# A fourth weight slot, a first stage over two token tiles, and later bf16 stores in a fused decoder layer

## The reference

```python
p = x @ w_in      # columns: [B_a | C_a | v_a | val_b | gate_b | g_a | g_b], 1024 each
y_a = (B_a * conv3_causal(C_a * v_a)) @ w_out_a
u   = conv31_causal(val_b * sigmoid(gate_b)) + conv_b_bias
y_b = silu(LN(u)) @ w_out_b
mix = (sigmoid(g_a) * y_a + sigmoid(g_b) * y_b) @ w_o
x1  = LN(alpha * x + mix)
x2  = LN(alpha * x1 + relu(x1 @ w_up)**2 @ w_down)      # output, float32
```

## Time and profile before

| | us |
|---|---|
| median of the runs shown (2359.38, 2360.63, 2711.35) | 2360.63 |
| the profiled execution's own time | 2351.3 |
| its span on the slowest core, number 6 | 2349.8 |
| spans of the 8 cores | 2327.6 to 2349.8 |
| PE busy | 2189.2 (93%) |
| DVE, ACT, POOL busy | 825.3, 901.7, 561.7 |

### The profile page before, as it was taken

The page is one execution under the profiler, slowest core; times in us unless marked ns, Lnnn a source line. Parts: engine busy times, 40 slices in busy tenths (PEclk is TensorE's granted clock), DMA queues, the critical chain, the costliest instruction groups (busy, mean ns, idle before and its releaser), DMA issues.

```text
span 2349.8 us, 33231 instructions; the slowest of 8 cores (2327.6 to 2349.8 us)
## 1 busy us (share of the span) xinstructions
PE 2189.2 (93%) x11616; PEld 968.0 (41%) x11616; DVE 825.3 (35%) x1200; ACT 901.7 (38%) x1424; POOL 561.7 (24%) x501
## 2 busy tenths in 40 slices
PE   5787899989999999999999999999999999999796
PEld 2333344333444434434444444444444444444342
DVE  2342360313703246122542237132461336322403
ACT  1132155222563225522354324723255324642552
POOL 0022041421405303132313214033031323040221
PEclk9899999999999999999999999999999999999898
DMA  9978879798677976657644665447644475444352
GB/s 169 220 207 174 206 164 172 175 243 215 154 198 182 260 216 177 187 175 237 202 151 147 203 199 190 145 157 218 211 155 144 151 225 191 157 152 171 119 187 90
DMA packets 109108, 428.42 MB, mean 182 GB/s; under 512 B 12944, under 2 KB 54160, under 8 KB 66448
## 3 DMA queue, kind: packets, MB, share of 16 engines
q1 hardware_dynamic: 84240, 318.21, 41.6%
q0 software_dynamic: 15488, 91.30, 21.4%
q10 hardware_dynamic: 9216, 16.78, 1.9%
HBM read 437.31 MB, written 63.44 MB: 213 GB/s over the span
## 4 chain that ended last, share of the span: by engine, by line
PE 76%; DMA 17%; DVE 2%; issue 2%; ACT 1%; POOL 1%; SPq 0%; POOLq 0%; DVEq 0%; ACTq 0%
PE ps L260 72%; DMA wsl<-wblk 8%; DMA wbf<-wsl 5%; PE ps L378 4%; DMA rep<-u0d 2%; DMA xft<-xblk 1%; POOL tt L270 1%; DVE res L283 1%; DMA wsl<-wbf 1%; DVE sbf L270 0%; ACT rstd L266 0%; SPq L108 0%; DVE sgt L283 0%; DVE tt L270 0%; DVE rstd L283 0%
## 5 line engine op out<-in xcount | busy, mean ns | idle before, releaser
L260 PE MATMUL ps<-xbf,wsl 128*128 128x512 bf16 x3648 | 844.8, 387 | 71.0 <-DMA wsl<-wblk 58.8
L260 PE MATMUL ps<-bx,wsl 128*128 128x512 bf16 x2560 | 572.5, 381 | 3.0 <-DMA wsl<-wblk 2.8
L260 PEld LDWEIGHTS ps<-xbf,wsl 128*128 128x128 bf16 x3648 | 356.0, 99 | 524.3 <-issue 127.6
L260 PE MATMUL ps<-h,wsl 128*128 128x512 bf16 x2496 | 549.6, 381 | 17.5 <-DMA wsl<-wblk 17.5
L266 ACT ACTIVATE tA<-ps 128x512 f32<-128x512 f32 x448 | 266.3, 595 | 511.2 <-PE ps L260 470.6
L260 PEld LDWEIGHTS ps<-bx,wsl 128*128 128x128 bf16 x2560 | 249.6, 98 | 312.7 <-issue 19.1
L260 PEld LDWEIGHTS ps<-h,wsl 128*128 128x128 bf16 x2496 | 244.5, 98 | 317.6 <-issue 28.3
L270 POOL TENSOR_TENSOR tt<-tt,rstd 128x512 f32<-128x512 f32 x180 | 246.5, 1370 | 97.9 <-ACT rstd L266 75.3
L270 POOL TENSOR_TENSOR tt<-res,mu 128x512 f32<-128x512 f32 x112 | 152.6, 1363 | 462.3 <-DMA yblk<-tt 219.9
L266 ACT ACTIVATE sq<-res 128x512 f32<-128x512 f32 x112 | 69.9, 630 | 412.5 <-DVE res L283 412.5
L270 POOL TENSOR_TENSOR tt<-u,mu 128x512 f32<-128x512 f32 x68 | 92.0, 1354 | 507.6 <-ACT mu L266 452.3
(11 more groups left out here) (54 smaller groups left out, 1010.5 us busy)
## 6 DMA issues: line engine op xcount, KB each, us to landing
wsl<-wbf SPq DMA_DIRECT2D x225, 1024.0 KB, 5.2
wsl<-wblk POOLq DMA_DIRECT2D x63, 1024.0 KB, 11.8
wbf<-wsl SPq DMA_DIRECT2D x36, 1024.0 KB, 12.3
rep<-u0d SPq DMA_DIRECT2D x256, 135.0 KB, 4.1
xft<-xblk POOLq DMA_DIRECT2D x64, 256.0 KB, 7.6
yblk<-tt ACTq DMA_DIRECT2D x64, 256.0 KB, 6.9
u0d<-u SPq DMA_DIRECT2D x64, 136.0 KB, 3.9
xbf<-xblk POOLq DMA_DIRECT2D x8, 1024.0 KB, 12.9
```

Of the source, the lines that this page charges most:

```text
L260: last = e.matmul(bank_ap, lhsT=l, rhs=r, start=(start and idx == 0), stop=(stop and idx == n - 1))
```

## The change

- **Slots.** `NS` is 4: loads are issued up to n+3. The space comes from `u0`, whose 8 tiles with halo give way to 3 tiles in rotation (`NU`) and 2 small halo tiles, and from `sbf`, 4 tiles to 2. `u0d` holds all tokens of a channel in one row, so that the halo of pass i+1 is what pass i wrote; the DVE copy of the halo goes.
- **First stage.** `stage_F_start` runs the F work of passes 0 and 1 on one loading of the B0 blocks, with conv(0, 0 to 5) in between. The first x tile and the first block are loaded in halves, and 16 matmuls on the first halves come first. conv(0, 6), conv(0, 7) and the layer norm of pass 0 go into `stage_S1A(0)`. Pass 0 has no F stage and no B0 loads.
- **Stores.** The 26 other blocks are stored at passes 1 to 3, by a table: 8, 12 and 6. Float32 reads in passes 0 to 3: 26, 26, 18, 6, that is 76 instead of 53.
- **Mix sums.** `stage_mix` uses `Stats`: 14 additions on DVE instead of 8, 2 matmuls instead of 8. The 2 are issued after S1A's first tile (in the last pass, after the first late DN block).
- **Last pass.** `LATE` is 3. `ln1_apply` there writes the residual on DVE. The statistics of pass 6 are issued behind f = 1 of `stage_up`.
- **End.** `ln2_last` works in place instead of through `tt`, subtracts for 5 tiles before it needs 1/sigma, and issues the outputs on SP's queue.

```diff
-NS = 3
+NS = 4
+NU = 3
...
-        LATE = 2
+        LATE = 3
         seq = [B0 + k for k in range(4)] + [A0 + k for k in range(6)]
         for i in range(NPASS):
-            if i < NPASS - 1:
+            if 0 < i < NPASS - 1:
                 seq += [B0 + k for k in range(4)]
...
+        STORE_PASS = (2, 1, 2, 3, 2, 1, 2, 3, 1, 2, 3, 1, 2)
...
-            return blk % 3
+            k = blk - S30 if blk < A0 else blk - UP0 + 10
+            return STORE_PASS[k % 13]
...
+        def F_gate(i, j, bv, bgk):
+            r = rt("sgt", 2)
+            act(sgt[r][:], ps[bgk][:, :], AF.Tanh, reads=[("ps", bgk)], writes=[("sgt", r)], scale=0.5)
+            ru = rt("u0", NU)
+            stt(u0[ru][:], sgt[r][:], 1.0, ps[bv][:, :], ALU.add, ALU.mult,
+                reads=[("ps", bv), ("sgt", r)], writes=[("u0", ru)])
+            rel(bv, bgk)
+            S.dma("sp", udsem[i % 2][j], u0d[j, :, HL + i * T:HL + (i + 1) * T], u0[ru][:],
+                  reads=[("u0", ru)], writes=[("u0d", i % 2, j)])
...
+        def stage_F_start():
+            for m in range(4):
+                s = w_next(B0 + m)
+                js = (2 * m, 2 * m + 1)
+                if m == 0:
+                    bks = [(nb(), nb()) for _ in js]
+                    for j, pair in zip(js, bks):
+                        for which, b in enumerate(pair):
+                            mm(ps[b][:, :], [(wk(s, kc, 2 * j + which), xbf[0][:, kc, :]) for kc in range(4)],
+                               reads=["w0a", "x0a"], writes=[("ps", b)], start=True, stop=False)
+                    for j, pair in zip(js, bks):
+                        for which, b in enumerate(pair):
+                            mm(ps[b][:, :], [(wk(s, kc, 2 * j + which), xbf[0][:, kc, :]) for kc in range(4, 8)],
+                               reads=[("wsl", s), ("xbf", 0)], writes=[("ps", b)], start=False, stop=True)
+                        F_gate(0, j, *pair)
+                        F_halo(j, s)
+                    for j in js:
+                        bv, bgk = nb(), nb()
+                        F_mm(1, j, s, bv, bgk)
+                        F_gate(1, j, bv, bgk)
+                        if j == 1:
+                            spread(0, 0)
+                else:
+                    for j in js:
+                        for i in range(2):
+                            bv, bgk = nb(), nb()
+                            F_mm(i, j, s, bv, bgk)
+                            F_gate(i, j, bv, bgk)
+                            if i == 0:
+                                F_halo(j, s)
+                        if j == 2:
+                            spread(0, 1)
+                        conv(0, j - 2, stC)
...
             if j + NREP < 8:
                 spread(i, j + NREP)
+            elif i == 0:
+                spread(1, j + NREP - 8)
...
+                if late:
+                    tsc("dve", buf[:, e_, :], tt[r][:], pv[:, 3, e_:e_ + 1], pv[:, 4, e_:e_ + 1],
+                        ALU.mult, ALU.add, reads=[("tt", r), "cst"], writes=[(bid, e_)])
...
+        def ln2_last(i, R):
+            buf, bid = R
+            eng = ["pool" if e_ % 3 == 2 else "dve" for e_ in range(7)] + ["pool"]
+
+            def sub(e_):
+                tten(eng[e_], buf[:, e_, :], buf[:, e_, :], mu[1][:], ALU.subtract,
+                     reads=[(bid, e_), ("mu", 1)], writes=[(bid, e_)])
+
+            order = [0, 2, 1, 5, 3, 7, 4, 6]
+            for e_ in (0, 2, 1, 5, 3):
+                sub(e_)
+            for n, e_ in enumerate(order):
+                if e_ in (7, 4, 6):
+                    sub(e_)
+                tten(eng[e_], buf[:, e_, :], buf[:, e_, :], rstd[1][:], ALU.mult,
+                     reads=[(bid, e_), ("rstd", 1)], writes=[(bid, e_)])
+                act(buf[:, e_, :], buf[:, e_, :], AF.Identity, reads=[(bid, e_), "cst"],
+                    writes=[(bid, e_)], bias=pv[:, 6, e_:e_ + 1], scale=pv[:, 5, e_:e_ + 1])
+                S.dma("sp", osem[n % NTT], yblk[i, :, e_, :], buf[:, e_, :],
+                      reads=[(bid, e_)], writes=[("y", i, e_)])
...
-                if e_ % 2 == 0:
-                    prev = (e_, q)
-                else:
-                    p, pq = prev
-                    rs = bf16_sum((rbuf[:, p, :], rbuf[:, e_, :]), [(rid, p), (rid, e_)])
-                    rq = bf16_sum((sq[pq][:], sq[q][:]), [("sq", pq), ("sq", q)])
-                    pend.append((e_ // 2, rs, rq))
...
+                if prev is not None:
+                    st_.take(*prev)
+                prev = (e_, rbuf[:, e_, :], (rid, e_), sq[q][:], ("sq", q))
+            st_.take(*prev)
...
+        stage_F_start()
+        lnc_tasks = [(lambda j=j: lnc_apply(j)) for j in range(8)]
         for j in range(8):
             stage_S1A(0, True, j)
-            conv(0, j, stC)
+            if j < 2:
+                conv(0, 6 + j, stC)
+            elif j == 2:
+                stC.finish(0)
+            else:
+                take(lnc_tasks, 2 if j < 6 else 1)
+        ln_flush()
...
+                if last and f == 1:
+                    stD.finish(1)
```

More of the change, by code:

```diff
@@ L152, in build_nc @@
         apre = sb("apre", [128, 8, T], BF16)
-        u0 = sb("u0", [128, 8, HL + T], BF16)
+        u0 = [sb(f"u0_{i}", [128, T], BF16) for i in range(NU)]
+        u0h = [sb(f"u0h{i}", [128, HL], BF16) for i in range(2)]
         u = sb("u", [128, 8, T], F32)
@@ L157, in build_nc @@
         sumQ = [sb(f"sumQ{i}", [128, T], F32) for i in range(2)]
-        sbf = [sb(f"sbf{i}", [128, T], BF16) for i in range(4)]
+        sbf = [sb(f"sbf{i}", [128, T], BF16) for i in range(2)]
         mu = [sb(f"mu{i}", [128, T], F32) for i in range(2)]
@@ L227, in w_next @@
                 S.dma("sp", castsem[expect], wbf[expect], wsl[n % NS][:],
-                      reads=[("wsl", n % NS)], writes=[("wbf", expect)])
+                      reads=[("wsl", n % NS)] + (["w0a"] if n == 0 else []),
+                      writes=[("wbf", expect)])
             return n % NS
@@ L291, in wk, with F_mm, F_halo, stage_F @@
             return wsl[s][:, kc * 512 + q * 128: kc * 512 + (q + 1) * 128]
-        def stage_F(i, first, each=None):
-            xb = xbf[i % 2]
+        def F_gate(i, j, bv, bgk):
[7 more added lines that the diff above has]
+                  reads=[("u0", ru)], writes=[("u0d", i % 2, j)])
+        def F_mm(i, j, s, bv, bgk):
+            q0 = (j % 2) * 2
+            for which, b in ((0, bv), (1, bgk)):
+                mm(ps[b][:, :], [(wk(s, kc, q0 + which), xbf[i % 2][:, kc, :]) for kc in range(8)],
+                   reads=[("wsl", s), ("xbf", i % 2)], writes=[("ps", b)])
+        def F_halo(j, s):
+            q0 = (j % 2) * 2
+            hv, hg = nb(), nb()
+            for which, b in ((0, hv), (1, hg)):
+                mm(ps[b][:, 0:HL], [(wk(s, kc, q0 + which), xhbf[:, kc, :]) for kc in range(8)],
+                   reads=[("wsl", s), "xhbf"], writes=[("ps", b)])
+            rh = rt("hsm", 4)
+            act(hsm[rh][:], ps[hg][:, 0:HL], AF.Tanh, reads=[("ps", hg)], writes=[("hsm", rh)], scale=0.5)
+            ru = rt("u0h", 2)
+            stt(u0h[ru][:], hsm[rh][:], 1.0, ps[hv][:, 0:HL], ALU.add, ALU.mult,
+                reads=[("ps", hv), ("hsm", rh)], writes=[("u0h", ru)])
+            rel(hv, hg)
+            S.dma("sp", uhsem[j], u0d[j, :, 0:HL], u0h[ru][:], reads=[("u0h", ru)],
+                  writes=[("u0dh", j)])
+        def stage_F(i, each):
             s = None
@@ L298, in stage_F @@
                     s = w_next(B0 + j // 2)
-                q0 = (j % 2) * 2
                 bv, bgk = nb(), nb()
[L301 to L318, removed]
@@ L531, in stage_mix @@
                    start=True, stop=False)
[L533 to L537, removed]
             prev = None
@@ L650, in build_nc, with f_each @@
         MER = (h, "h")
[L652 to L653 removed]
+        stage_F_start()
+        lnc_tasks = [(lambda j=j: lnc_apply(j)) for j in range(8)]
         for j in range(8):
             stage_S1A(0, True, j)
[L656 removed]
+            if j < 2:
+                conv(0, 6 + j, stC)
+            elif j == 2:
+                stC.finish(0)
+            else:
+                take(lnc_tasks, 2 if j < 6 else 1)
+        ln_flush()
         ln2_tasks = []
[L659 removed]
         for i in range(NPASS):
             last = i == NPASS - 1
[L662 to L675 removed]
+            if 0 < i < NPASS - 1:
+                def f_each(j):
+                    take(ln2_tasks, 1 if j % 2 else 0)
+                stage_F(i + 1, f_each)
             for e_ in range(4):
@@ L726, in build_nc @@
                 stD.finish(1)
-                for e_ in range(8):
-                    ln_flush(1)
-                    ln_fin.append(ln2_apply(i, R, e_, "pool" if e_ % 3 == 2 else "dve"))
-                ln_flush()
+                ln2_last(i, R)
             else:
```

83 lines of the change are left out of this document (32 added, 51 removed).

## The result

Four runs of the changed kernel took 2326.8 to 2336.1 us, median 2332.1, against 2350.4 to 2360.6 us for the kernel before. The ratio is 0.9894, with a 95% interval of 0.9853 to 0.9935: 1.1% faster, 25 us, where 88 were forecast and the range ended at 2325. (Executions far above the others of their kernel, as the 2711.35 us of the kernel before, are left out of all ratios: where their clocks are on record, one die or both ran at a lower one.) The profiled executions differ by less, since that of before was within 1 us of its fastest and that of after was its slowest: their spans are 2349.8 and 2334.6 us.

The account below looks back on a forecast made before the run. The start was taken as bound by transfers, the middle by PE, passes 0 to 2 by something between. Gains of 33 + 36 + 0 + 13 + 6 = 88 us gave 2263 from the profiled 2351.3 (2273 from the median); range 2240 to 2325.

Parts of the forecast that it names:

- Prices of transfers: All-engine time per transfer: 6.45 us a casting load, 3.2 a bf16 block or store; said to hold within 4%.
- slower rival: Casting loads cost some 9 us each in the busy passes; kernel at 2371 us, chance 0.05.
- From need to loss: Passes 0 to 3: transfer need against PE time turned into losses totalling 32 us; 36 us gained.
- the line with three slots: Passes 0 to 3: losses read from the old kernel's transfer shares; new shares would lose 96 us together.
- rate, not slots: Rival for passes 0 to 3: the line of losses holds, passes lose 96 us; kernel at 2337 us, chance 0.13.
- Start: Stretch before S3 of pass 0: S3 begins at 153 instead of 186.5 us; 33 us gained, bounds 22 and 43.
- Mix sums: Mix stage: six matmuls less and six DVE additions more net minus 1 to plus 3 us a pass; taken as 0.
- Late blocks and end: Last pass: a third late DN block and shared work gain 13 us; its end, with fewer waits, gains 6.

Follow-up runs that it names:

- e4: The changed kernel with three weight slots and eight u0 tiles in rotation; 1.0039 of the kernel before.
- e3: The changed kernel with the 26 blocks stored at passes 0 to 2 as before; 0.9785 of the kernel before.
- e13: The changed kernel with the ten B0 and A0 blocks stored at their second use instead of their first; 0.9982 of the kernel before.
- e14: The changed kernel with the edits of e3, e5, e6, e7 and e13 and the mix sums as before the change; 0.9827 of the kernel before.
- e5: The changed kernel with the halo of pass 0 written in one transfer with its u0 tile; 0.9905 of the kernel before.
- e6: The changed kernel with subtract and multiply of pass 0's convolution layer norm on DVE instead of POOL; 0.9874 of the kernel before.
- e9: The changed kernel with each conv of pass 0 two tiles later; no ratio, times 2338.8 and 2334.0 us.
- e10: The changed kernel with the third and fourth weight loads held until pass 1's first u0 tile is made; 0.9875 of the kernel before.
- e7: The changed kernel with the load of x for the pass after next issued behind stage_mix's own loads; 0.9793 of the kernel before.

## Why the prediction was wrong

*Prices of transfers: right.* Needs of 213, 260, 247 and 188 us were forecast for passes 0 to 3; the windows give 0.82 x 256.8 = 211, 0.86 x 300.3 = 258, 0.85 x 288.5 = 245, 0.70 x 279.4 = 196. Had a float32 read cost 9 us, as the slower rival had it, pass 1 would need 260 + 26 x 2.55 = 326 us, more than the 300.3 it took. (By the same step that rival's 331 us for pass 0 of before are 254 + 66 = 320, still over the 306 there.) By the estimate from the rate in the Trainium skill ("HBM Reference", Specifications) pass 1's transfers would have hidden in 238 us. They did not: the engines were busy for 258, and the measured pass decides.

*From need to loss: the first step that failed, 10 us for 36.* The text put losses of 5, 17, 10 and 0 us where the line with three slots gave 22, 37, 30 and 7. Cut on core 6 they were 13, 29, 17 and 8, of which the mix sums are up to 3 each. e4 gives the line for three slots by measurement: p1 and p2 of 305 and 307 are losses of 33 and 35, near the 37 and 30 of the line, and p3 loses 11 for 7; p0 loses 7 by the mark, where the line had 22 (against the same 243.9 and 271.6). Together that is 86 for 96, so but for pass 0 the line was sound. The stores' move to passes 1 to 3 costs 20 to 26 us (e3), near the 28 of the line (96 less 68). What was mis-sized is the worth of the fourth slot: 33 us over the four passes, not the 64 between 96 and 32. The forecast had netted the two into "36 us gained"; measured apart they are a gain of 33 and a loss of 23.

The "rate, not slots" rival, put at 0.13, came nearest with 2337, but by luck. It let the slot be worth nothing, which e4 refutes, and kept the 33 us of the start, which did not come: two errors of 30 to 40 us that cancel.

*Start: the second step that failed, 5 us for 33 (9 by S3's first matmul).* Two terms were compared, 151 us of transfers and 143 of PE, and the later taken with 2 us on top. The transfers took 0.89 x 178.9 = 159 us, 8 over the 151. But the start was not the later of two: in the changed kernel the transfers were busy for 0.89 of it (0.85 between 20 and 117 us) and PE for 126 of 179 us. The likely reason, argued and not shown, is that each holds up the other: PE stands 16 us before a conv whose `rep` lands late, with weight slots in its hands, and POOL can't issue the next load. That the ten stores matter is shown (e13, e14: S3 9 to 17 us earlier), though not whether by their amount. That no single wait of those tried does is shown by e4, e5, e6, e9 and e10. In e13, core 6 has 0.83 x 162.4 = 135 us of transfers, not the 127 that 159 less 32 would give:

```profile
0.00:162.40 162.40, 126.73 (x970) 57.98 (x970) 69.07 (x112) 40.10 (x73) 34.03 (x44) 0.96 0.83 151
```

One term the text had at nothing: the wait for `apre` at S3, a median of 5.3 us after the change, 4.2 in e13 and 8.9 to 11.4 in e9. How the rest of the 27 us that e13 has beside its transfers divides among the halo's write, its read back and the weights was not settled.

*Mix sums: right within the bounds, 1.5 us a pass for 0.* The wait of 4.0 to 4.7 us was 5.9 in pass 4. The text's own numbers gave more than the 0 it took: a wait of 4.0 to 4.7 in place of 0.32 and 1.71, less 1.3 for the matmuls, is 0.7 to 1.4 a pass. Left out was the clock: after the wait PE's next matmuls run at the lower of its two levels, the two on the sums in 1.19 us for 0.59 and the four behind them in 1.91, and the window of pass 4 has a granted clock of 0.98 for 1.00. And the 2.73 us wait for x, which I counted as room for the additions, mattered more: with its cause moved (e7) the kernel gained more than the sums had cost. In the changed kernel three requests for x follow at once (the fifth, sixth and seventh tile), DVE has the first 9.5 us after its request instead of 7, and the additions come after it.

*Late blocks and end: 9 and 3 for 13 and 6.* PE still waits 4.42 us for the end of the layer norm, since DVE, not ACT, is now last; ACT itself waits for it:

```profile
2200.24 0.81 ACT L275 ACTIVATE bx<-tt,pv_s 128x512 bf16<-128x512 f32 x1 [1.32 <-DVE tt L279]
2201.20 6.47 PE L269 MATMUL ps<-bx,wsl 128*128 128x512 bf16 x22 [4.42 <-ACT bx L275]
```

At the end DVE's steps beside POOL took 1.4 and 1.7 us each, not 0.75. The last row is one without POOL beside it:

```profile
2316.81 2.94 POOL L279 TENSOR_TENSOR u<-u,mu 128x512 f32<-128x512 f32 x2 [55.70 <-ACT mu L275]
2317.87 4.09 DVE L279 TENSOR_TENSOR u<-u,mu 128x512 f32<-128x512 f32 x3
2321.88 5.09 DVE L279 TENSOR_TENSOR u<-u,rstd 128x512 f32<-128x512 f32 x3
...
2326.89 0.68 DVE L279 TENSOR_TENSOR u<-u,mu 128x512 f32<-128x512 f32 x1
```

The text had named this ("if DVE is slow because POOL reads beside it, the lower end holds") for the late blocks; it holds at both places, and both values lie in their bounds (8 to 16, 3 to 8). The Trainium skill ("SBUF — State Buffer", SBUF: two separate sides) says of a DVE instruction with two SBUF inputs that it and a reading POOL instruction lock each other out; these rows agree with it: alone, the same steps take 0.69.

*As a whole.* All terms missed to the same side, four of them inside their bounds. By the cuts the start missed its term by 28 us, passes 0 to 3 by 26, the sums by 10, the late blocks and the end by 4 and 3: together 71, where the ratio has 63. The range ended at 2325 because it cut off half of the rate case; the sum of the lower bounds was never made.

## What to carry to other kernels

When a change buys a buffer and spends it on more traffic, forecast the two apart: here the fourth slot gave 33 us and the later stores took 20 to 26 back, and the table that was there before was the better one. A wait that precedes added work is to be asked for its cause before it is counted as room for that work; moving one load behind the others' was worth as much as the whole change. And where transfers and an in-order engine hold up each other, neither count of busy time bounds the stretch from above: take the share that the trace of before shows over the whole stretch (0.89 up to S3, before the change and after), and test a suspected wait by removing it, since the chain of waits names only the last of several.

## What the hardware showed that I had not expected

A write of 128 x 64 bytes took 23.46 us to land while float32 loads were queued, longer than one of 128 x 1088 bytes at the same place (16.38 us in e5). DVE's fp32 `tensor_scalar` on SBUF tiles took 0.54 us in the late blocks (the median of eight, the longest 1.48), less than the 0.69 of the two-input steps from which it had been priced.
